# Two low halves of weights per block boundary on GpSimd, first input halves in two pieces, another order on VectorE and ScalarE

## The reference, cut to what matters

```python
def first_block(...):
    ...
        x = x + mod[:, 2, None] * mix_x
        h2 = modulate(rmsnorm(x, g_ffn[l]), mod[:, 3, None], mod[:, 4, None])
        x = x + mod[:, 5, None] * swiglu(h2, w_up[l], w_down[l])
    return rmsnorm(x, g_final)

def second_block(x, ...):
    for i in range(DEPTH_2):
        g = norm_g[i]
        f = swiglu_2(rms_norm(x, g[0]), ffn_w_in[i, 0], ffn_w_out[i, 0])
        x = x + FFN_RESIDUAL_WEIGHT * rms_norm(f, g[1])
        h = rms_norm(x, g[2])
        m = stick_breaking_attention(...) if i % 2 == 0 else multi_head_latent_attention(...)
        x = x + rms_norm(m, g[3])
        f = swiglu_2(rms_norm(x, g[4]), ffn_w_in[i, 1], ffn_w_out[i, 1])
        x = x + FFN_RESIDUAL_WEIGHT * rms_norm(f, g[5])
    return x
```

## Time and profile before

| what | value |
|---|---|
| median of 3 runs | 1461.66 us (1460.35 to 1462.11) |
| the profiled execution | 1462.73 us, its span 1461.5 us |
| TensorE busy | 1430.4 us (98%) |
| VectorE busy | 864.6 us (59%) |
| ScalarE busy | 763.5 us (52%) |
| GpSimd busy | 39.6 us (3%) |
| mean granted clock of TensorE | 0.995 |
| chain that ended last | TensorE 90%, VectorE 5%, ScalarE 2% |

### The profile page before, as it was taken

How to read it: one execution, slowest core, us unless ns; L and a number is a source line. 1 busy time by engine, 2 the same in 40 slices (tenths; PEclk the granted TensorE clock), 3 DMA queues, 4 the chain that set the end, 5 groups by cost and what they waited for, 6 DMA issues and landing times.

```text
span 1461.5 us, 19637 instructions
## 1 busy us (share of the span) xinstructions
PE 1430.4 (98%) x8066; PEld 1203.1 (82%) x8066; DVE 864.6 (59%) x1207; ACT 763.5 (52%) x1102; POOL 39.6 (3%) x72
## 2 busy tenths in 40 slices
PE   7999999999999999999999999999999999999998
PEld 5999889978888788888987888887888879888886
DVE  3628866775554755546465655557555475765553
ACT  4436355555544645445685655446554476755442
POOL 0000100000000000000241000000000000000000
PEclk8999999999999999999999999999999999999999
DMA  9437666455555555555534555555555542355552
GB/s 381 138 104 298 249 238 218 160 177 182 186 189 187 197 184 186 185 190 192 177 116 137 170 185 189 186 191 185 185 187 190 181 173 73 115 187 184 191 187 88
DMA packets 69930, 267.34 MB, mean 183 GB/s; under 512 B 7760, under 2 KB 8016, under 8 KB 66384
## 3 DMA queue, kind: packets, MB, share of 16 engines
q1 hardware_dynamic: 67680, 259.13, 51.9%
q10 hardware_dynamic: 2160, 6.95, 1.4%
HBM read 265.00 MB, written 1.05 MB: 182 GB/s over the span
## 4 chain that ended last, share of the span: by engine, by line
PE 90%; DVE 5%; ACT 2%; DMA 1%; issue 1%; SPq 0%; POOL 0%; DVEq 0%; ACTq 0%
PE PS L730 24%; PE PS L746 14%; PE PS L748 14%; PE PS L747 14%; PE PS L373 5%; PE PS L374 4%; PE PS L375 4%; PE PS L714 2%; PE PS L405 1%; PE PS L406 1%; PE PS L407 1%; DMA MC<-in_mod 1%; PE PS L474 1%; DVE WL L1669 1%; DVE TN L2116 1%
## 5 line engine op out<-in xcount | busy, mean ns | idle before, releaser
L1669 DVE TENSOR_TENSOR WL<-RAW,WH 128x1024 fp32r<-128x1024 f32 (+1 forms) x440 | 532.4, 1222 | 307.6 <-ACT WH L1102 306.9
L1102 ACT ACTIVATE WH<-RAW 128x1024 fp32r<-128x1024 f32 (+1 forms) x440 | 454.6, 1054 | 294.9 <-DMA RAW<-in_up 174.7
L746 PE MATMUL PS<-WH,XH 128*128 128x512 f32 (+1 forms) x928 | 381.4, 411 | 9.2 <-DVE XL L2124 9.0
L748 PE MATMUL PS<-WH,XL 128*128 128x512 f32 (+1 forms) x928 | 362.7, 391 | 0.0
L747 PE MATMUL PS<-WL,XH 128*128 128x512 f32 (+1 forms) x928 | 362.4, 391 | 0.0
L746 PEld LDWEIGHTS PS<-WH,XH 128*128 128x128 f32 x928 | 174.6, 188 | 59.5 <-DVE XL L2124 13.9
L748 PEld LDWEIGHTS PS<-WH,XL 128*128 128x128 f32 x928 | 174.6, 188 | 37.1
L747 PEld LDWEIGHTS PS<-WL,XH 128*128 128x128 f32 x928 | 175.3, 189 | 27.8
L730 PE MATMUL PS<-WH,GH 128*128 128x512 f32 x440 | 137.4, 393 | 0.0
L730 PE MATMUL PS<-WH,GL 128*128 128x512 f32 x440 | 135.7, 390 | 0.0
L730 PE MATMUL PS<-WL,GH 128*128 128x512 f32 x440 | 135.7, 390 | 0.0
(11 more groups left out here) (348 smaller groups left out, 1851.1 us busy)
## 6 DMA issues: line engine op xcount, KB each, us to landing
RAW<-in_up SPq DMA_DIRECT2D x220, 512.0 KB, 4.6
RAW<-in_down SPq DMA_DIRECT2D x110, 512.0 KB, 3.2
RAW<-in_win SPq DMA_DIRECT2D x44, 512.0 KB, 6.4
RAW<-in_mod SPq DMA_DIRECT2D x16, 1024.0 KB, 6.9
MC<-in_mod SPq DMA_DIRECT2D x8, 1024.0 KB, 13.8
RAW<-in_sbqk SPq DMA_DIRECT2D x16, 512.0 KB, 4.7
GROW<-in_grow ACTq DMA_DIRECT2D x9, 512.0 KB, 4.8
RAW<-in_wo SPq DMA_DIRECT2D x8, 512.0 KB, 4.1
```

The costliest lines, as they stand in the source:

```text
L746: e.matmul(o_[:, 0:n], l, w[:, s], start=(k == 0), stop=False, skip_group_check=True)
L748: m = e.matmul(o_[:, 0:n], ll, w[:, s], start=False, stop=(k == KD - 1), skip_group_check=True)
L1102: e.activation(WH[s][:, 0:c], RAW[s][:, 0:c], ACT.Copy).then_inc(*sig("hi", j))
L1669: e.tensor_tensor(WL[s][:, 0:c], RAW[s][:, 0:c], WH[s][:, 0:c].bitcast(F32), ALU.subtract).then_inc(*sig("lo", j))
```

## The change

GpSimd makes the low halves of chunks c0 + 3 and c0 + 4 of each of the seven boundaries (14 subtractions), with a semaphore of its own; VectorE leaves them out. The first half z of the input is rounded and subtracted in two pieces of two blocks of 128 columns each, and steps 0 and 1 of the next block wait for one piece each. VectorE's and ScalarE's orders within a boundary are new.

```diff
+        ENTRY = [chunk[k] for k in (("up", 0), ("up", UP), ("sbv", 0), ("up", UP * FFN[3]), ("up", UP * FFN[4]),
+                                    ("mla", 0), ("up", UP * FFN[6]))]
+        BY_POOL = {c0 + i for c0 in ENTRY for i in (3, 4)}
...
-            return WH[slot[j]], WL[slot[j]], at("lo", j)
+            return WH[slot[j]], WL[slot[j]], at("pool lo" if j in BY_POOL else "lo", j)
...
-                        pe.wait_ge(*at("xl", v, h, c // 2))
+                        pe.wait_ge(*at("xl", v, h, min(c, 2)))
...
-                e.activation(XH[:, 4 * z:4 * z + 4, h * P:(h + 1) * P], four(TN.of(("tn", b, h, z))[:, :]),
-                             ACT.Copy).then_inc(*sig("xh", b, h, z))
+                for q, n in ((2, 4),) if z else ((0, 2), (1, 2)):
+                    e.activation(XH[:, 2 * q:2 * q + n, h * P:(h + 1) * P],
+                                 four(TN.of(("tn", b, h, z))[:, :])[:, 2 * q - 4 * z:2 * q - 4 * z + n, :],
+                                 ACT.Copy).then_inc(*sig("xh", b, h, q))
...
                 if b < 7:
                     split(c0 + 6)
+                    turned(b, 1, 0)
+                    turned(b, 1, 1)
                     if b:
                         scale_of_input(b, 0)
-                    turned(b, 1, 0)
-                    turned(b, 1, 1)
...
-                    if plan[j][0] == "mod":
+                    if plan[j][0] == "mod" or j in BY_POOL:
...
-            def turned(b, h, z):
-
-                s = (slice(4 * z, 4 * z + 4), slice(h * P, (h + 1) * P))
-                dv.wait_ge(*at("xh", b, h, z))
+            def turned(b, h, q):
+
+                n, o = (4, 4) if q == 2 else (2, 2 * q)
+                s = (slice(o, o + n), slice(h * P, (h + 1) * P))
+                dv.wait_ge(*at("xh", b, h, q))
...
+            def split(b):
+
+                for j in (ENTRY[b] + 3, ENTRY[b] + 4):
+                    s, c = slot[j], plan[j][2]
+                    po.wait_ge(*at("hi", j))
+                    e.tensor_tensor(WL[s][:, 0:c], RAW[s][:, 0:c], WH[s][:, 0:c].bitcast(F32),
+                                    ALU.subtract).then_inc(*sig("pool lo", j))
...
+            for b in range(3):
+                split(b)
             for pr in range(1, 9):
...
+            for b in range(3, 7):
+                split(b)
```

More of the change, by code:

```diff
@@ L813, in sv_step @@
                 n, c = p // 4, p % 4
-                pe.wait_ge(*at("xl", 2, h, c // 2))
+                pe.wait_ge(*at("xl", 2, h, min(c, 2)))
                 m = narrow(("sv", n, h), "sbv", p, h, ("svc", n, h), c == 0, c == 3)
@@ L828, in first_heads @@
                 rows_spread(2)
-                pair("sbqk", 0, ("sqk", 0), ("qk", 0, 1), XH, XL, at("xl", 2, 1, 1))
+                pair("sbqk", 0, ("sqk", 0), ("qk", 0, 1), XH, XL, at("xl", 2, 1, 2))
             lagged(KD, sv_step, 2, None, first_heads)
@@ L870, in pe_program @@
                 if 1 <= pr < 8:
-                    pair("sbqk", pr, ("sqk", pr), ("qk", pr, 1), XH, XL, at("xl", 2, 1, 1))
+                    pair("sbqk", pr, ("sqk", pr), ("qk", pr, 1), XH, XL, at("xl", 2, 1, 2))
                 if pr == 8:
@@ L903, in mla_step @@
             def mla_step(p, h):
-                pe.wait_ge(*at("xl", 5, h, p // 2))
+                pe.wait_ge(*at("xl", 5, h, min(p, 2)))
                 m = narrow(("mp", h), "mla", p, h, ("cn", h, 3), p == 0, p == 3, n=MW)
@@ L1377, in boundary @@
                 root(b, 0)
[L1378 to L1383, removed]
+                if b < 7:
                     split(c0 + 4)
@@ L1386, in boundary @@
                 square_of(b, 1, 0)
-                if b < 6:
+                if b < 7:
                     turned(b, 0, 1)
@@ L2050, in dve_program, with updates @@
             scale_of("vf", 40, S_GFFN, 32, 0, 8)
-            def updates(b, h):
+            def updates(b, h, *parts):
                 (banks, end), (grow, come) = block_end(b, h), rows_of(b)
@@ L2058, in updates @@
                     dv.wait_ge(*at("mod", 12 * b + 11))
-                for n in (1, 0):
+                for n in parts:
                     y, before = Y.take(("y", b, h, n), ("xa" if b < 2 else "x", b, h, n))
@@ L2103, in scaled @@
             def scaled(b, h, z):
-                tn, before = TN.take(("tn", b, h, z), ("xl", b, h, z))
+                tn, before = TN.take(("tn", b, h, z), ("xl", b, h, 2 if z else 1))
                 k0 = 4 * z
@@ L2118, in scaled @@
                 m.then_inc(*sig("tn", b, h, z))
-            def turned(b, h, z):
-                s = (slice(4 * z, 4 * z + 4), slice(h * P, (h + 1) * P))
-                dv.wait_ge(*at("xh", b, h, z))
-                e.tensor_tensor(XL[:, s[0], s[1]], four(TN.of(("tn", b, h, z))[:, :]), XH[:, s[0], s[1]].bitcast(F32),
-                                ALU.subtract).then_inc(*sig("xl", b, h, z))
+            def turned(b, h, q):
+                n, o = (4, 4) if q == 2 else (2, 2 * q)
+                s = (slice(o, o + n), slice(h * P, (h + 1) * P))
+                dv.wait_ge(*at("xh", b, h, q))
+                e.tensor_tensor(XL[:, s[0], s[1]], four(TN.of(("tn", b, h, q // 2))[:, :])[:, o % 4:o % 4 + n, :],
+                                XH[:, s[0], s[1]].bitcast(F32), ALU.subtract).then_inc(*sig("xl", b, h, q))
             def scale_of_input(b, h):
@@ L2138, in boundary @@
             def boundary(b, c0, between=None):
-                updates(b, 0)
+                updates(b, 0, 1, 0)
                 if b == 6:
@@ L2142, in boundary @@
                 added(b, 0)
-                if b < 2:
-                    split(c0 + 3)
                 sum_of(b, 0)
@@ L2148, in boundary @@
                 renewed(b, 0, 1)
-                if b == 6:
+                if b < 7:
                     split(c0 + 2)
@@ L2152, in boundary @@
                     turned(b, 0, 0)
+                    turned(b, 0, 1)
                     scaled(b, 0, 1)
[L2154 to L2163, removed]
+                    updates(b, 1, 1)
+                    turned(b, 0, 2)
+                    updates(b, 1, 0)
+                else:
+                    updates(b, 1, 1, 0)
                 added(b, 1)
                 sum_of(b, 1)
-                if b < 7:
-                    split(c0 + 4)
                 inverse(b, 1)
@@ L2171, in boundary @@
                 if b < 7:
[L2172 to L2181, removed]
-                        scale_of_input(b, 0)
[L2183 to L2188, removed]
+                    scaled(b, 1, 0)
+                    scaled(b, 1, 1)
+                    turned(b, 1, 0)
+                    split(c0 + 5)
+                    turned(b, 1, 1)
+                    turned(b, 1, 2)
+                    if b:
+                        scale_of_input(b, 0)
                     if b == 5:
+                        scale_of_latents(0)
                         between()
```

## The result

The changed kernel takes 1472.62 us (median of 4 runs, 1471.1 to 1473.05) against 1461.01 us of the kernel before in the same comparison: ratio 1.0076, 95% interval 1.0064 to 1.0087. It is **slower by 11.6 us**, 0.8%, and 5.1 us above the upper end of the range.

A forecast was written before the change was run, and what follows sets the result against it. TensorE was taken as the bound, its waits at seven boundaries worth some 15 us at most. Boundaries 0 to 6: +1.4, +1.4, -0.7, +0.5, -0.7, -2.8, -1.1, sum -2.0; forecast 1459.7 us, range 1452.5 to 1467.5.

The forecast's parts named there:

- the shutting out: GpSimd reading SBUF blocks VectorE instructions with two SBUF inputs, and the reverse; 1.93 us per GpSimd subtraction.
- the places at boundaries 1 and 3: GpSimd's subtractions delay the second sum and `XL` at boundary 1 (+1.4 us), `XL` at boundary 3 (+0.5 us).
- I take 2.08 us: Price of one GpSimd subtraction of 1024 columns, scaled from a 0.26 us mask of 128 columns.
- no gain is left at 2.35: Price per GpSimd subtraction, in us, at which the whole change gains nothing; from 2.6 it is slower by more than 2.9.
- The walk of part 2: Boundary by boundary, GpSimd's 14 subtractions and their blocking of VectorE turn part 1's -8.7 us into -2.0.
- Boundary 5: GpSimd is done before `XL` is due: At boundary 5 GpSimd blocks nothing; -1.35 and -1.45 for the clock make -2.8 us.
- `scale_of_input` moves behind `XH`; ... I cost at nothing.: On ScalarE; a gate needs the moved result some 3 us later, so the move costs nothing.
- the wait before half 1: At boundary 5 TensorE still waits 1.2 us before the first step of half 1.
- The wait of 0.72 goes whole: At boundary 6 `XL` has a step more of cover, so TensorE's wait goes; -1.1 us there.
- Part 1 alone: -8.7 us.: Pieces and new orders with GpSimd's work free: -7.2 us over the boundaries, 1.5 us from the clock at boundary 5.
- Rival C: Slower, chance 0.25: GpSimd's second input costs more; at 3.1 us each +10, 1471.7 us; sign: mean above 2.6.
- the second `X<-X,Y` of boundary 1: Half 0's second sum, held by GpSimd, is drawn at about 2.6 us; TensorE idles 1.5 us before L704.

The follow-up runs named there:

- e13: The changed kernel with GpSimd filling the 14 low halves with zeros instead of subtracting, as in e9, and the orders of e11; 1456.88 us.
- e9: The changed kernel with GpSimd filling the 14 low halves with zeros instead of subtracting; 1460.63 us, ratio 0.9995.
- e7: The changed kernel with the order edits of e1 and e2 together, GpSimd's 14 subtractions kept; 1471.22 us.
- e5: The changed kernel with VectorE making the 14 subtractions again and the order edits of e1 and e2; 1459.28 us.
- e2: The changed kernel with `scale_of_input` of half 0 back ahead of half 1's `TN`, `XH` and `XL` on both engines; 1472.04 us.
- e1: The changed kernel with ScalarE at boundary 6 again rounding both `XH` of half 0 before the `WH` of c0 + 4; 1471.03 us.
- e8: e7 with GpSimd at boundaries 0 and 1 waiting until the second `X<-X,Y` of half 0 is done; 1469.39 us.
- e10: The changed kernel with each GpSimd subtraction in four instructions of 256 columns; 1466.6 us, ratio 1.0039.
- e11: e5 with VectorE's reciprocal of half 0's scale behind half 1's last `XL`, except at boundary 5; 1456.86 us, ratio 0.9972.

## Why the prediction was wrong

By the medians the change splits into three: pieces, orders and relief, mended, -4.7 us (e13); the slips of order +3.7 (e9 against e13); GpSimd's subtractions in place of fills +12.6 (the changed kernel's +11.6 against e9's -1.0). The sum is +11.6; I had -8.7, 0 and +6.7. The middle term is not all order: the table shows 2.3 of it, and the rest fits the clock behind boundary 5, which e9's profiled execution escaped; of its other executions no trace exists. The mechanism that bounds it, the shutting out, was right, and so were the places at boundaries 1 and 3. Its sizes and what I costed at nothing were wrong. For the first size, a subtraction of the changed kernel that nothing held (boundary 0):

```profile
295.57 2.38 POOL L2429 TENSOR_TENSOR WL<-RAW,WH 128x1024 fp32r<-128x1024 f32 x1 [3.08 <-ACT WH L1106]
```

The steps, one by one:

- **"I take 2.08 us".** A subtraction that nothing holds took 2.38 us (the row above; the second ones of boundaries 2, 4 and 6 took 2.36 to 2.38). The mean of 2.57 includes waiting for VectorE. By my own scale no gain is left at 2.35, so this is worth 2.3 us. The Trainium skill's "GPSIMD Engine Reference", section "Elementwise — side-by-side cycle accounting", from which I had estimated 2.25, was nearer than my value from the mask, 5% under the measured 2.38.
- **The walk of part 2** went from 6.7 (9.0 with the right price) to 12.6 measured. It left out that a two-input instruction of one column is shut out as well (boundary 6, which I gave no lock cost and where e7 lies 1.9 us above e5), the slow matmuls behind the late turn of boundary 1, and the second subtraction at boundaries 2, 4 and 5 (e7 against e5: 1.0, 1.3 and 0.6 us, I had 0.5, 0.5 and 0). "Boundary 5: GpSimd is done before `XL` is due" was wrong: in the changed kernel its first subtraction there held the second new `x` (2.70 us instead of 0.75) and its second ran to 1184.13, while `XL` was due at 1183.41. Boundary 0 came as forecast, by luck of arrival (e2).
- **"`scale_of_input` moves behind `XH`; ... I cost at nothing."** The gate was not late. But the squares and the root (1.5 us) now stand ahead of ScalarE's next `WH`, so `WL` came late at boundaries 1 to 3, and at boundary 5 the latents came 2.12 us late. I had looked at who needs the moved result, not at what queues behind it. At boundary 5 the wait before half 1 did shrink to 1.28, as forecast (1.2), and the latents took it back; with the old order (e13) it stays at 2.50. In no run were both on time.
- **"The wait of 0.72 goes whole"** (boundary 6). I took the removed exception for a mere simplification. By itself it costs little (e9, -0.6 although `XH` was late); together with the lock, which then falls on `XL`, and with the matmuls at half clock behind it, it cost 2.7 us (e1).
- **"Part 1 alone: -8.7 us."** e13 has -0.1, -0.7, -0.9, -1.1, -0.9, -0.3, -0.8 against my -0.1, -1.0, -1.2, -1.3, -1.2, -2.8, -1.1: 0.3 too much at each of five boundaries, and 2.5 at boundary 5, where in e13 neither wait nor slow matmuls went. In the changed kernel the slow matmuls did go, as forecast, and the latents took the gain; e1, with the same waits, has them again, so that was in part luck.
- **Rival C** named 1471.7, but with a price of 3.1 us. The number was near, the reason was not: at 2.38 my walk gave no change. The group's mean of 2.57 lay just under its sign, 2.6.
- **Right**: the second `X<-X,Y` of boundary 1, forecast drawn at about 2.6, took 2.8 (3.48 less the first one's 0.64), with TensorE late at the turn by 2.04 where I had 1.5; TensorE never waited for GpSimd's `WL` in the changed kernel.

## What to carry to other kernels

Work moved to an idle GpSimd is not free when it reads SBUF: it can take VectorE away for the rest of the GpSimd instruction under way, when VectorE's own next instruction reads SBUF (two inputs in most places here, one in e8), so price it as an interruption of VectorE's critical chain at the worst moment, and if it must be, cut it into short instructions (e10 gave back 6 us of 11.6). For every instruction that is moved, list what now stands behind it on its engine, not only who needs its result. And when a change takes several steps at once, time the steps alone: here the order was worth 4.8 us and the offloading cost more than twice that.

## What the runs showed that I had not expected

The lock holds very short instructions too: one column with two SBUF inputs waited 1.6 us (e1). And it holds the one-input `XN`, for nearly a whole subtraction in e8; in e2, where GpSimd's had half a microsecond left to run, the two took 1.21 instead of 0.88 us. The subtraction that followed in e2, begun while the second `XN` ran, took 2.66 instead of 2.38, so GpSimd seems to wait as well; that was not tried.

Four quarters with nothing in their way take 2.80 us where one whole takes 2.38, so a cut costs 0.14 us.

The clock behind equal pauses was not the same in each run. The changed kernel and e1 have the same code at boundary 5 and the same waits, 1.28 and 2.12 us. Of the changed kernel and then of e1, from the second wait on:

```profile
1196.90:1199.90 3.00, 3.00 (x16) 1.00 0.91 305
1196.90:1199.90 3.00, 3.00 (x11) 0.50 0.82 324
```

The boundary cost 0.1 and 1.6 us. TensorE stood 2.25 us at boundary 5 in both e5 and e11. Of e5:

```profile
1182.00:1185.00 3.00, 2.65 (x13) 1.00 0.08 20
```

and of e11:

```profile
1182.00:1185.00 3.00, 3.00 (x10) 0.51 0.18 23
```

In this pair it costs 0.6 us (-1.0 against -0.5), less than in the other, because e5 then waits 0.35 us for `CN` and e11 does not. What decides between full and half clock was not tried and stays open. It scatters the times of one kernel by more than a microsecond, so a single profiled execution can hide or feign a gain of that size.
